# Re-ordering the five engine programs at the stage boundaries of a three-layer float32 network, and the distance at which weight splits run ahead

## What is computed

```
for layer in (0, 1):
    x = x + rms_norm(mixer(rms_norm(x)))          # layer 0: pooling and 31-tap convolution; layer 1: 3-tap convolution
    x = x + rms_norm(relu(rms_norm(x) @ W1)**2 @ W2)     # 2048 -> 8192 -> 2048
h = rms_norm(x); proj = h @ w_in                  # layer 2: attention and spatial gating
x = x + merged(proj) @ w_out
```

## Time and profile before

| | |
|---|---|
| median of 3 runs | 2830.99 us (2829.72 to 2831.48) |
| profiled execution: device time | 2828.28 us |
| its span in the trace | 2826.6 us |
| PE matmul busy | 2744.9 us, 97% |
| PE weight loads busy | 2269.0 us, 80% |
| DVE, ACT, POOL busy | 57%, 47%, 11% |
| weights and the rest read from HBM | 511.47 MB, 182 GB/s |

### The profile page before, as it was taken

One profiled execution on the slowest core, in us unless ns is written; L12 is line 12 of the kernel. 1 busy time (PEld: TensorE's weight loads), 2 busy tenths in 40 slices (PEclk: granted clock), 3 DMA queues, 4 the chain that ended last, 5 costly groups with the idle time before them and its releaser, 6 DMA issues.

```text
span 2826.6 us, 30637 instructions
## 1 busy us (share of the span) xinstructions
PE 2744.9 (97%) x12357; PEld 2269.0 (80%) x12357; DVE 1616.5 (57%) x1705; ACT 1334.4 (47%) x1649; POOL 314.9 (11%) x328
## 2 busy tenths in 40 slices
PE   8888899999999989999999999999998999999999
PEld 6767788888888878888778888888887888888887
DVE  4998654555555565555554555555556557654454
ACT  5765544444444445444354444444445546544442
POOL 3963100000000010000100000000011101000000
PEclk9999999999999999999999999999999999999999
DMA  7444555555555545555455555555554654455554
GB/s 242 134 150 148 173 186 192 188 193 186 193 192 181 193 150 207 180 193 194 149 194 193 193 183 190 193 192 185 189 187 144 202 190 164 164 193 194 194 179 149
DMA packets 259183, 515.55 MB, mean 182 GB/s; under 512 B 8114, under 2 KB 10724, under 8 KB 258532
## 3 DMA queue, kind: packets, MB, share of 16 engines
q1 hardware_dynamic: 259044, 513.60, 54.2%
HBM read 511.47 MB, written 2.10 MB: 182 GB/s over the span
## 4 chain that ended last, share of the span: by engine, by line
PE 91%; DVE 6%; issue 1%; ACT 1%; SPq 0%; DMA 0%; POOL 0%; POOLq 0%; DVEq 0%; ACTq 0%
PE bank L621 29%; PE bank L623 29%; PE bank L622 29%; DVE conv_out L1446 3%; DVE w_lo L607 2%; PE bank L668 2%; DMA w_raw<-in_ab_w_in 0%; DVE A_lo L1245 0%; ACT A_hi L912 0%; PE bank L684 0%; ACT w_hi L600 0%; ACT conv_in L1164 0%; PE bank L796 0%; PE bank L854 0%; DVE B_lo L1231 0%
## 5 line engine op out<-in xcount | busy, mean ns | idle before, releaser
L607 DVE TENSOR_TENSOR w_lo<-w_raw,w_hi 128x1024 fp32r<-128x1024 f32 x960 | 1215.3, 1273 | 991.6 <-ACT w_hi L600 988.3
L600 ACT ACTIVATE w_hi<-w_raw 128x1024 fp32r<-128x1024 f32 x960 | 1013.1, 1060 | 1082.0 <-PE bank L623 1041.4
L621 PE MATMUL bank<-w_hi,A_lo 128*128 128x512 f32 x2432 | 962.4, 396 | 49.1 <-DVE A_lo L1245 19.9
L623 PE MATMUL bank<-w_hi,A_hi 128*128 128x512 f32 x2432 | 953.4, 392 | 0.0
L622 PE MATMUL bank<-w_lo,A_hi 128*128 128x512 f32 x2432 | 952.8, 392 | 0.0
L621 PEld LDWEIGHTS bank<-w_hi,A_lo 128*128 128x128 f32 x2432 | 460.6, 189 | 151.3 <-issue 42.5
L621 PE MATMUL bank<-w_hi,B_lo 128*128 128x512 f32 x1408 | 552.0, 392 | 15.7 <-DVE B_lo L1231 11.5
L622 PE MATMUL bank<-w_lo,B_hi 128*128 128x512 f32 x1408 | 549.3, 390 | 0.0
L623 PE MATMUL bank<-w_hi,B_hi 128*128 128x512 f32 x1408 | 549.2, 390 | 0.0
L623 PEld LDWEIGHTS bank<-w_hi,A_hi 128*128 128x128 f32 x2432 | 459.9, 189 | 97.3
L622 PEld LDWEIGHTS bank<-w_lo,A_hi 128*128 128x128 f32 x2432 | 460.6, 189 | 93.3
(11 more groups left out here) (143 smaller groups left out, 839.4 us busy)
## 6 DMA issues: line engine op xcount, KB each, us to landing
w_raw<-in_ffn_w SPq DMA_DIRECT2D x256, 1024.0 KB, 5.0
w_raw<-in_w_in SPq DMA_DIRECT2D x88, 1024.0 KB, 5.0
w_raw<-in_sc_w_in SPq DMA_DIRECT2D x48, 1024.0 KB, 5.2
w_raw<-in_ab_w_in SPq DMA_DIRECT2D x24, 1024.0 KB, 5.1
w_raw<-in_ab_w_out SPq DMA_DIRECT2D x16, 1024.0 KB, 5.0
w_raw<-in_sc_w_out SPq DMA_DIRECT2D x16, 1024.0 KB, 5.0
w_raw<-in_w_out SPq DMA_DIRECT2D x16, 1024.0 KB, 5.4
w_raw<-in_w_proj_a SPq DMA_DIRECT2D x8, 1024.0 KB, 5.0
```

Of the source, the lines that this page charges most:

```text
L600: e.activation(w_hi[:, s % SPLIT_SLOTS, :], raw, ACT.Copy).then_inc(hi_made, 1)
L607: e.tensor_tensor(w_lo[:, slot, :], raw, w_hi[:, slot, :].bitcast(F32), ALU.subtract).then_inc(lo_made, 1)
L621: e.matmul(ps, lo[:, kt, tok], wh, start=first, stop=False)
L623: ins = e.matmul(ps, hi[:, kt, tok], wh, start=False, stop=last)
```

## The change

- AHEAD becomes 3: the work of step s stands behind the splits up to s + 3. In the first four steps of a stage the bound is still SPLIT_SLOTS - 1.
- At a boundary a tile's 512 channels are transposed in two halves of two transposes, each with its own auxiliary bank and its own signals, so that A_hi and A_lo follow half by half, and a step waits for its own half.
- PE transposes (0, 0) and (1, 0) ahead of the last held step of tile 1, (0, 1) ahead of step 3 of tile 0, and (1, 1) ahead of step 0 of tile 1.
- ACT issues hi of f + 2 and f + 3 ahead of the tile (0, 0), and hi of f + 4 and f + 5 ahead of (0, 1). DVE updates x for (0, 0) and (1, 0) together, ahead of lo of f + 2, and has lo of f + 3 between the updates of tile 1.
- POOL does the root of tile 0, then the last gain of tile 0 once lo of f + 2 is made, then the root of tile 1, and the last gain of tile 1 once x has its piece (1, 1).

```diff
@@ -40,7 +40,7 @@
 Z_SLOTS = 3
 TAP_SLOTS = 5
 STEP_K = 2
-AHEAD = SPLIT_SLOTS - 1
+AHEAD = 3
 SCRATCH = 1024
 TAPS_PER_STEP = 6
 
@@ -148,7 +148,7 @@
 
 def pre_fills(p):
 
-    return [("pre", p, g, tt) for tt in range(NT) for g in range(2)] + \
+    return [("pre", p, g, tt, h) for tt in range(NT) for g in range(2) for h in range(2)] + \
            [("pre", p, g, h) for g in range(2, NG) for h in range(2)]
 
 
@@ -585,7 +585,7 @@
             for s in range(first, end - HELD):
                 upto = s + AHEAD
                 if stage > 0 and s < first + HELD:
-                    upto = min(upto, first + AHEAD)
+                    upto = min(upto, first + SPLIT_SLOTS - 1)
                 split_to(e, one, at, min(upto, end + SPLIT_SLOTS - HELD - 1))
                 yield SEQ[s]
             split_to(e, one, at, end + SPLIT_SLOTS - HELD - 1)
@@ -624,17 +624,16 @@
             if done is not None:
                 ins.then_inc(done, 1)
 
-        def halves_key(c, g, tt):
-
+        def halves_key(c, i, tt):
+
+            g = chunks[c].group0 + i * STEP_K // GK
             key = chunks[c].halves(g)
-            return key + ((tt,) if key[0] == "pre" and key[1] > 0 and g < 2 else (1,))
+            return key + ((tt, i % 2) if key[0] == "pre" and key[1] > 0 and g < 2 else (1,))
 
         def wait_step(e, c, i, which):
-            ch, s = chunks[c], POS[c, i]
-            e.wait_ge(lo_made, s + 1)
-            if i % 2 == 0:
-                g = ch.group0 + i * STEP_K // GK
-                e.wait_ge(lo_cast.sem, max(lo_cast.of(*halves_key(c, g, tt)) for tt in which))
+            e.wait_ge(lo_made, POS[c, i] + 1)
+            if i % 2 == 0 or i < HELD:
+                e.wait_ge(lo_cast.sem, max(lo_cast.of(*halves_key(c, i, tt)) for tt in which))
             if i == 0 and c >= 2:
                 for tt in which:
                     sem, value = taken(c - 2, tt)
@@ -678,11 +677,12 @@
             def turn_tile(p, g, tt):
 
                 e.wait_ge(x_made.sem, x_made.of(p - 1, g, tt))
-                b4 = aux_begin("pre", p, g, tt)
-                for k in range(GK):
-                    f = g * CH + k * P
-                    ins = e.transpose(b4[:, k * P:(k + 1) * P], x[:, tt, f:f + P], ident)
-                ins.then_inc(aux_filled("pre", p, g, tt), 1)
+                for h in two:
+                    b4 = aux_begin("pre", p, g, tt, h)
+                    for k in two:
+                        f = g * CH + (2 * h + k) * P
+                        ins = e.transpose(b4[:, k * P:(k + 1) * P], x[:, tt, f:f + P], ident)
+                    ins.then_inc(aux_filled("pre", p, g, tt, h), 1)
 
             def held_steps(c, which, done=None):
                 for i in range(n_steps[c] - HELD, n_steps[c]):
@@ -696,15 +696,17 @@
                 for i in range(n_steps[c] - HELD, n_steps[c]):
                     if i == n_steps[c] - 1:
                         turn_tile(p, 0, 0)
+                        turn_tile(p, 1, 0)
                     step_matmuls(e, c, i, (1,), step_done)
-                for tt in tiles:
-                    if tt == 1:
+                for i in range(HELD):
+                    if i == HELD - 1:
                         turn_tile(p, 0, 1)
-                    for i in range(HELD):
-                        if i == 2:
-                            turn_tile(p, 1, tt)
-                        wait_step(e, f, i, (tt,))
-                        step_matmuls(e, f, i, (tt,), step_done if tt == 1 else None)
+                    wait_step(e, f, i, (0,))
+                    step_matmuls(e, f, i, (0,), None)
+                turn_tile(p, 1, 1)
+                for i in range(HELD):
+                    wait_step(e, f, i, (1,))
+                    step_matmuls(e, f, i, (1,), step_done)
 
             def turn_z(slot, *key):
                 turn(lambda tt, f: z[:, slot, tt, f], *key)
@@ -906,12 +908,14 @@
 
             def hi_tile(p, g, tt):
 
-                e.wait_ge(aux_filled.sem, aux_filled.of("pre", p, g, tt))
-                for k in range(GK):
-                    kt = GK * g + k
-                    ins = e.activation(halves["A"][0][:, kt, tt * P:(tt + 1) * P], aux_bank("pre", p, g, tt)[:, k * P:(k + 1) * P],
-                                       ACT.Copy, scale=par_col(PRE_COL[p], kt))
-                ins.then_inc(hi_cast("pre", p, g, tt), 1)
+                for h in two:
+                    b4 = aux_bank("pre", p, g, tt, h)
+                    e.wait_ge(aux_filled.sem, aux_filled.of("pre", p, g, tt, h))
+                    for k in two:
+                        kt = GK * g + 2 * h + k
+                        ins = e.activation(halves["A"][0][:, kt, tt * P:(tt + 1) * P], b4[:, k * P:(k + 1) * P],
+                                           ACT.Copy, scale=par_col(PRE_COL[p], kt))
+                    ins.then_inc(hi_cast("pre", p, g, tt, h), 1)
 
             def hi_plain(buf, group, *key):
                 for h in two:
@@ -946,14 +950,12 @@
 
                 f = S0[STAGE[p]]
                 squares(p - 1, NG - 1, 0)
-                split_to(e, split_hi, at, f + 2)
+                split_to(e, split_hi, at, f + 3)
                 hi_tile(p, 0, 0)
-                split_to(e, split_hi, at, f + 3)
+                hi_tile(p, 1, 0)
                 squares(p - 1, NG - 1, 1)
-                hi_tile(p, 1, 0)
-                split_to(e, split_hi, at, f + 4)
+                split_to(e, split_hi, at, f + 5)
                 hi_tile(p, 0, 1)
-                split_to(e, split_hi, at, f + 5)
                 hi_tile(p, 1, 1)
 
             def early(p, c, i):
@@ -1239,12 +1241,13 @@
 
             def lo_tile(p, g, tt):
                 hi, lo = halves["A"]
-                e.wait_ge(hi_cast.sem, hi_cast.of("pre", p, g, tt))
-                for k in range(GK):
-                    kt, tok = GK * g + k, slice(tt * P, (tt + 1) * P)
-                    ins = e.scalar_tensor_tensor(lo[:, kt, tok], aux_bank("pre", p, g, tt)[:, k * P:(k + 1) * P],
-                                                 par_col(PRE_COL[p], kt), hi[:, kt, tok].bitcast(F32), ALU.mult, ALU.subtract)
-                ins.then_inc(lo_cast("pre", p, g, tt), 1)
+                for h in two:
+                    e.wait_ge(hi_cast.sem, hi_cast.of("pre", p, g, tt, h))
+                    for k in two:
+                        kt, tok = GK * g + 2 * h + k, slice(tt * P, (tt + 1) * P)
+                        ins = e.scalar_tensor_tensor(lo[:, kt, tok], aux_bank("pre", p, g, tt, h)[:, k * P:(k + 1) * P],
+                                                     par_col(PRE_COL[p], kt), hi[:, kt, tok].bitcast(F32), ALU.mult, ALU.subtract)
+                    ins.then_inc(lo_cast("pre", p, g, tt, h), 1)
 
             def lo_plain(buf, group, *key):
                 hi, lo = halves[buf]
@@ -1295,22 +1298,21 @@
                 finish(p - 1, NG - 1, 0, alone)
                 settle(p - 1, 0)
                 update(p - 1, 0, 0)
+                update(p - 1, 1, 0)
                 split_to(e, split_lo, at, f + 2)
                 lo_tile(p, 0, 0)
-                update(p - 1, 1, 0)
                 finish(p - 1, NG - 1, 1, alone)
-                split_to(e, split_lo, at, f + 3)
                 lo_tile(p, 1, 0)
                 settle(p - 1, 1)
                 update(p - 1, 0, 1)
+                split_to(e, split_lo, at, f + 3)
+                update(p - 1, 1, 1)
                 lo_tile(p, 0, 1)
-                update(p - 1, 1, 1)
-                split_to(e, split_lo, at, f + 4)
                 lo_tile(p, 1, 1)
                 for g in (2, 3):
+                    split_to(e, split_lo, at, f + 2 + g)
                     for tt in tiles:
                         update(p - 1, g, tt)
-                    split_to(e, split_lo, at, f + 5)
 
             def early(p, c, i):
                 if (c, i) == (STAGE[p] + 1, 0):
@@ -1618,10 +1620,12 @@
                 for n in range(NG - 1):
                     for tt in tiles:
                         gain(p, n, tt)
-                for tt in tiles:
-                    root(1, "postroot", "post", p, tt)
-                for tt in tiles:
-                    gain(p, NG - 1, tt)
+                root(1, "postroot", "post", p, 0)
+                e.wait_ge(lo_made, S0[STAGE[p + 1]] + 3)
+                gain(p, NG - 1, 0)
+                root(1, "postroot", "post", p, 1)
+                e.wait_ge(x_made.sem, x_made.of(p, 1, 1))
+                gain(p, NG - 1, 1)
                 root(NT, "rs", "pre", p + 1)
 
 
```

## The result

The kernel with the change takes 2781.23 us (median of 4 runs, 2780.84 to 2782.14), the one before 2830.78 beside it (2829.72 to 2831.48): a ratio of 0.9826, 95% interval 0.9809 to 0.9843. It is 49.5 us faster; 2783.0 was predicted, with 2774 to 2799 as the range. The profiled execution took 2780.84 us, with a span of 2779.1.

A forecast was written before the change was run, and what follows sets the result against it. PE's matmuls were taken as the bound, with gains only where PE waits or runs at half clock. 37.4 + 11.2 - 5.1 + 4.1 - 0.3 = 47.3 us off gave 2781.0 or 2783.7 by base; 2783 was said, range 2774 to 2799.

The forecast's parts named there:

- The gaps at the boundaries: Four boundaries: transposes issued earlier close all four PE waits for A_lo at each, 9.35 us a boundary, 37.4 us off.
- The rival of a boundary covered in part: Boundaries: links late again, half of the 37.4 and 11.2 us stays, 24 us more, 2807 us; chance 0.09.
- the one by which nothing is gained: Whole kernel: gaps closed on PE open on DVE instead, time within 0.2%; chance 0.02.
- The clock: Behind the boundaries: seven half-clock stretches of PE vanish once it stays fed, 11.2 us off.
- the rival in which it falls all the same: Boundaries: remaining short waits still bring the half clock, 7 x 1.6 us, 2794 us; chance 0.08.
- The splits before the boundary: Held steps after stages 0, 1 and 3: split of f - 1 comes late, 1.7 us each, 5.1 us lost.
- POOL: Boundaries: tile 0's gain beside A_lo and `finish` costs DVE nothing, 0, with 4 us as upper bound.
- AHEAD 3 at the start: Start of stage 0: PE's waits of 3.28 and 0.5 us for A_lo go, 4.1 us off.
- AHEAD 3 among the taps: Stage 0's taps: DVE's work and the chunk 6 eviction wait unchanged, 0, at most 1.7 us gained.
- The rival by which stage 0 gains nothing: Stage 0: pooling branch late, 4.1 us not gained and 4 lost, 2791 us; chance 0.09.
- AHEAD 3 elsewhere: Chunk ends outside stage 0: three steps of cover hold, only chunk 136 is tight, 0.3 us lost.
- the slower rival: The 160 chunk ends: three steps of cover too short, PE starves, 2864 us at 0.5 us each; chance 0.03.

## Why the prediction was right

**The sum** (47.3 us, 47.5 measured). That it came so close is partly luck: the boundaries gave 1.0 us less than their terms and stage 0 1.1 more, and stage 0 differs by up to 3.6 us between executions of the same order. The mechanism of the large terms is what the runs bear out.

**The gaps at the boundaries** (37.4 us). Right, by the list of waits and the ledger: with distance 5, where the new wait is absent, the boundaries save 47.6 us in all, and less 1.6 for each of seven half-clock stretches that is 36.4. The chain laid out on the times of before came out within 0.4 us. After's DVE timeline has x (0, 0) start at 292.30, `finish` of tile 1 at 295.86 and x (0, 1) at 298.50:

```profile
292.30 1.42 DVE L1288 SCALAR_TENSOR_TENSOR x_res<-acc,small,x_res 128x512 f32<-128x512 f32 x2 [0.66 <-POOL small L1611]
293.64 1.22 DVE L607 TENSOR_TENSOR w_lo<-w_raw,w_hi 128x1024 fp32r<-128x1024 f32 x1
294.77 1.12 DVE L1248 SCALAR_TENSOR_TENSOR A_lo<-bank,par,A_hi 128x128 fp32r<-128x128 f32 x4
295.86 0.69 DVE L1274 TENSOR_TENSOR acc<-bank,acc 128x512 f32<-128x512 f32 x1
```

Each link can be laid beside the same operation in the earlier trace rows: 0.75 us an update (1.42 for two), 1.12 for four A_lo. The rival of a boundary covered in part falls, and so does the one by which nothing is gained, but the first was near. Halves undone, transposes a step later and POOL's contention each took 0.7 to 3.0 us from every boundary (3.6 at one, with the half clock): the chain had as little to spare as was said.

**The clock** (11.2 us). Right: no window at 0.50 near a boundary, and the rival in which it falls all the same is out. The waits left there are 1.4 us at most, with a step and more between them. Of what brings the drop back the variants show this much. In the kernels whose gaps at the boundaries are 2.4 us or less from start to start (the longest is in the one with distance 5 for f - 5 alone) no half-clock stretch stands there. In the kernel with POOL's old order the gap ahead of step 3 of tile 0 is 3.0 us at all four boundaries instead of 0.9, and one stretch came, behind the last. With distance 2 there is a gap of 3.0 us in the held steps of boundaries 1, 2 and 4, and a stretch behind the first two. In the kernel before the gaps are 3.3 us, twelve of them, with seven stretches. So the same gap was followed by the drop at one boundary and not at the next; what decides between them no run shows.

**The splits before the boundary** (-5.1 us). Right in size and in place: a wait for w_lo in the held steps at boundaries 1, 2 and 4, none at the third. It measures 1.4 us (1.63 from start to start instead of 0.23), and the whole effect 1.7, by the kernel with distance 5. The cause is the one given: the timelines of ACT and DVE after show that hi of f - 1, f and f + 1 go as one group behind the squares, and the w_lo behind them is drawn out by POOL's gains:

```profile
284.37 2.94 ACT L600 ACTIVATE w_hi<-w_raw 128x1024 fp32r<-128x1024 f32 x3
```

```profile
285.45 4.45 DVE L607 TENSOR_TENSOR w_lo<-w_raw,w_hi 128x1024 fp32r<-128x1024 f32 x3 [1.75 <-ACT w_hi L600]
289.82 0.68 DVE L1274 TENSOR_TENSOR acc<-bank,acc 128x512 f32<-128x512 f32 x1
```

`finish` of tile 0 follows at 289.82, 7.6 us behind the start of f - 4 (282.21), exactly as worked out (295.0 behind 287.4). Of the 0.3 us given to the late x (1, 0), 0.1 shows at the transposes (1.11 from the start of the last matmul to the next, at the third boundary 1.02), and 0.1 where PE starts again after its wait: 0.34 to the second matmul at 288.03 instead of 0.23.

**POOL** (0, upper bound 4 us). Right, for the reason given and thanks to the two waits in its program. The gain after stands beside A_lo and `finish` (POOL's timeline):

```profile
294.93 1.30 POOL L1617 TENSOR_TENSOR acc<-acc,gain_row 128x512 f32<-128x512 f32 x1 [2.67 <-DVE w_lo L607]
```

and the four A_lo at 294.77 took 1.12 us, as without a gain. Without either wait the bound came true: 3.9 and 3.8 us. The Trainium skill (SBUF — State Buffer, "Who interferes with whom") has it that a DVE instruction with two SBUF inputs contends with a GpSimd instruction that reads SBUF, and one with at most one SBUF input doesn't. All of these rows agree, with 1.0 us for an update or a w_lo beside a gain and nothing for A_lo and `finish`, which read one input from PSUM.

**AHEAD 3 at the start** (4.1 us). 3.2 measured; PE's wait of 3.28 us and the one of 0.5 behind it are gone. From step 1 to step 17 it is 4.3 us. 1.1 us of it went another way: PE came to its first step 0.2 us earlier, but stayed at the half clock (matmuls 0.43 apart) to 16.4 us and not to 14.1, so that it came to step 1 1.1 us later. The kernel with distance 5 and the old order of stage 0 had 17.1 there and began 0.9 us later. The kernels with whole tiles and without POOL's wait for f + 2, which start as the kernel after does, had some 14.2, and step 17 came 4.4 and 4.5 us earlier in them. So this differs from one execution to the next and isn't of the change.

**AHEAD 3 among the taps** (0, at most 1.7). Here the term was too small: 2.0 us came in the profiled execution. DVE's first tap starts at 68.25 instead of 71.39, its last four at 225.12 instead of 230.74, so the chain itself became 2.5 us shorter. The step that failed is "the eviction remains and starts no earlier, since PE waits for the same B_lo". The eviction of chunk 6 starts 5.6 us earlier, not the 3.1 that the first tap does (ACT's timelines, before and after):

```profile
206.01 1.09 ACT L943 ACTIVATE acc<-bank 128x512 f32<-128x512 f32 x2 [1.61 <-PE bank L623]
```

```profile
200.40 1.09 ACT L947 ACTIVATE acc<-bank 128x512 f32<-128x512 f32 x2 [6.17 <-PE bank L623]
```

PE waits for the same B_lo, but that B_lo itself comes 5.7 us earlier (DVE's timelines, before and after):

```profile
196.98 1.65 DVE L1231 SCALAR_TENSOR_TENSOR B_lo<-bank,par,B_hi 128x256 fp32r<-128x256 f32 x4
```

```profile
191.24 1.65 DVE L1233 SCALAR_TENSOR_TENSOR B_lo<-bank,par,B_hi 128x256 fp32r<-128x256 f32 x4
```

From the first tap to the end of this B_lo lie 127.2 us before and 124.6 after; from there to the eviction 7.4 and 7.5, so the 1.7 us for a step of PE at the full clock didn't come; and from the eviction to the end of the last tap 26.9 in both. All of the gain thus lies ahead of the B_lo. It comes with the distance: in the three profiled kernels with distance 5 among the taps that stretch is 127.2 us each time, in the ten with 3 it is 124.6 to 125.4. DVE has the same instructions in it, 96 of the taps' and 32 w_lo, but the first took 73.7 us instead of 75.7 (from start to start) and the second 47.7 instead of 48.3. A likely reason is POOL: a tap beside one of POOL's instructions takes 0.9 to 1.0 us and one alone 0.5, and POOL starts 95 instructions in that stretch where it started 100 before (95 in all ten kernels, 100 in all three). No experiment was made on this alone, so it stays open.

How much of it reaches the first boundary differs from one execution to the next: between step 17 and f - 4, five of the ten kernels gain 1.8 to 2.4 us and the other five 0.2 or nothing. So the 0 of the prediction isn't refuted as a number, but its reason is. The rival by which stage 0 gains nothing falls, with 2.2 to 5.8 us gained in all ten.

**AHEAD 3 elsewhere** (-0.3 us). Right, 0.3 in stage 4 and 0 in both MLPs, and the slower rival falls: with a distance of 2 the MLPs lose only 0.4 us each. What that kernel shows beside it is where the distance has its limit: in stages 0, 2 and 4, somewhere between 2 and 3 steps.

**The base.** The sum was laid on the profiled execution of the kernel before (2781.0) and on the median (2783.7), and 2783 said. The first was nearer: 2781.23 us was measured.

## What to carry to other kernels

Where PE transposes for itself, the transposes should stand a step of other matmuls ahead of the step that needs them, and all engines' programs be laid out on one time axis to see that each link is there in time: the new order, with the halves and POOL's two waits, gave 46 of the 49 us. The distance of run-ahead is not one number: where activations share the queue, a short one can gain (here 3 in stage 0, while 2 lost 8.9 us there), and where a stage ends, a split left until after the last chunk's work is wanted too soon; setting it stage by stage gave 5.6 us more than 3 throughout. On the last links of such a chain, one microsecond of another engine's access to the same memory counts in full, so an elementwise operation that nobody waits for is worth a wait.

## What the runs showed of the hardware that was not expected

- A GpSimd gain of 128x512 costs the DVE instruction beside it about 1.0 us in both forms measured: 1.02 us on an update of 0.75, 1.06 on a w_lo of 1.22. The gain itself takes 1.3 us alone or beside the update, and 1.7 beside the w_lo.
- The half clock at the start of the kernel lasts differently long from one execution to the next: until 14.1 us before, 16.4 after and 17.1 with distance 5, for a first matmul at 11.4, 11.2 and 12.2 us.
- One wait of 2.31 us of PE was enough at the start to bring the half clock at once: in the kernel with distance 5 the matmuls lie 0.43 apart from 24.40 to 27.39, behind the wait that ends at 23.52. The kernel before waited 3.28 us at the same place and stayed at the full clock. What tells the two apart isn't settled. Its PE timeline:

```profile
23.52 0.47 PE L621 MATMUL bank<-w_hi,A_lo 128*128 128x512 f32 x1 [2.31 <-DVE A_lo L1233]
...
24.40 0.63 PE L621 MATMUL bank<-w_hi,A_lo 128*128 128x512 f32 x1
```
